# A two-block transformer kernel: the first expert's tokens gathered by column halves, second-bias products moved behind expert two, a down-projection unit's parts moved ahead of conditioning work

## The reference

```
def swiglu(x, w_up, w_down):                      # feed-forward of the first block
    a, b = split(x @ w_up, 2)
    return (silu(a) * b) @ w_down

def moe_ffn(h, w_router, b_router, w1, b1, w2, b2):   # 32 experts, 4 for each token
    logits = h @ w_router + b_router
    top_v, top_e = top_k(logits, 4); weights = softmax(top_v)
    for each expert e and the tokens sent to it:
        hcat  = x[tok] @ w1[e] + b1[e]            # 1024 -> 2048
        act   = min(glu, 7) * sigmoid(1.702 * glu) * (clip(lin, -7, 7) + 1)
        y     = act @ w2[e] + b2[e]               # 1024 -> 1024
    out = sum over the 4 experts of weights * y
```

## Time and profile before

| | us |
|---|---|
| median of 3 runs | 2614.63 |
| lowest and highest of them | 2614.07, 2614.64 |
| the profiled execution | 2615.32 |
| span of its instructions | 2613.6 |
| PE busy | 2581.9 |
| DVE busy | 1295.6 |
| moved from and to HBM | 705 MB, mean 270 GB/s |

### The profile page before, as it was taken

How to read it: one execution, slowest core, us unless ns; L and a number is a source line. 1 busy time by engine, 2 the same in 40 slices (tenths; PEclk the granted TensorE clock), 3 DMA queues, 4 the chain that set the end, 5 groups by cost and what they waited for, 6 DMA issues and landing times.

```text
span 2613.6 us, 39337 instructions
## 1 busy us (share of the span) xinstructions
PE 2581.9 (99%) x15833; PEld 1899.0 (73%) x15833; DVE 1295.6 (50%) x1741; ACT 759.0 (29%) x1288; POOL 73.7 (3%) x95
## 2 busy tenths in 40 slices
PE   9999999999999999999999999999999999999998
PEld 9989898999999998999989888833333333333333
DVE  6866785687788768747844063312122121112112
ACT  4414441443343245323423143122121121121111
POOL 0010200000000120000001000000000000000000
PEclk9999999999999999999999999999999999999999
DMA  6685433456656834445554533899999999999999
GB/s 231 212 283 184 140 138 145 161 178 223 222 191 205 301 129 133 152 152 164 186 198 149 206 107 151 328 392 426 427 428 427 428 427 427 428 428 427 427 428 406
DMA packets 265659, 705.38 MB, mean 270 GB/s; under 512 B 13125, under 2 KB 155409, under 8 KB 215761
## 3 DMA queue, kind: packets, MB, share of 16 engines
q1 hardware_dynamic: 253520, 663.66, 65.9%
q0 software_dynamic: 9856, 36.41, 3.9%
q10 hardware_dynamic: 2176, 3.83, 0.4%
HBM read 699.61 MB, written 6.60 MB: 270 GB/s over the span
## 4 chain that ended last, share of the span: by engine, by line
PE 77%; SPq 12%; DMA 7%; DVE 2%; issue 1%; ACT 1%; DVEq 0%; ACTq 0%
PE acc L1824 8%; SPq L917 8%; PE acc L1089 6%; PE mix L1093 6%; PE acc L1091 6%; PE acc L1035 5%; PE acc L1162 5%; PE acc L1839 4%; PE acc L1629 4%; SPq L920 4%; PE mix L1083 4%; PE acc L1178 3%; PE acc L1061 2%; PE acc L1112 2%; PE acc L1421 2%; DMA big<-in_w 2%
## 5 line engine op out<-in xcount | busy, mean ns | idle before, releaser
L1089 PE MATMUL acc<-branch_parts,area_parts 128*128 128x256 f32 x1176 | 343.9, 292 | 0.4 <-DVE big_parts L2436 0.4
L1093 PE MATMUL mix<-big_parts,zz_parts 128*128 128x256 f32 x1176 | 332.8, 283 | 0.0
L1091 PE MATMUL acc<-area_parts,ring_parts 128*128 128x256 f32 x1176 | 332.4, 283 | 0.0
L3256 DVE COPY zz<-acc 128x512 f32<-128x512 f32 x32 | 22.1, 692 | 546.4 <-PE acc L1824 546.4
L2436 DVE TENSOR_TENSOR ring_parts<-ring,area_parts 128x1792 fp32r<-128x1792 f32 (+2 forms) x125 | 238.0, 1904 | 84.2 <-ACT area_parts L1982 61.0
L1089 PEld LDWEIGHTS acc<-branch_parts,area_parts 128*128 128x128 f32 x1176 | 225.0, 191 | 9.7 <-DVE big_parts L2436 1.2
L1091 PEld LDWEIGHTS acc<-area_parts,ring_parts 128*128 128x128 f32 x1176 | 225.1, 191 | 0.2
L1093 PEld LDWEIGHTS mix<-big_parts,zz_parts 128*128 128x128 f32 x1176 | 225.0, 191 | 0.0
L1982 ACT ACTIVATE area_parts<-ring 128x1792 fp32r<-128x1792 f32 (+1 forms) x116 | 189.6, 1634 | 16.6 <-DMA ring<-in_ffn_up 12.1
L2529 DVE SCALAR_TENSOR_TENSOR zz_parts<-area_parts,ring_parts 128x1792 fp32r<-128x1792 f32 x84 | 170.2, 2026 | 6.3
L1974 ACT ACTIVATE area<-acc 128x256 f32<-128x256 f32 (+1 forms) x66 | 32.5, 492 | 367.6 <-PE acc L1776 341.6
(11 more groups left out here) (553 smaller groups left out, 4740.2 us busy)
## 6 DMA issues: line engine op xcount, KB each, us to landing
ring<-in_ffn_up SPq DMA_DIRECT2D x86, 1024.0 KB, 5.0
big<-in_w SPq DMA_DIRECT2D x79, 1024.0 KB, 25.7
ring<-in_w SPq DMA_DIRECT2D x76, 1024.0 KB, 26.0
ring<-in_w_in SPq DMA_DIRECT2D x72, 1024.0 KB, 7.1
area<-in_w SPq DMA_DIRECT2D x57, 1024.0 KB, 26.3
spare<-in_w SPq DMA_DIRECT2D x38, 1024.0 KB, 25.6
area<-in_w_ada POOLq DMA_DIRECT2D x24, 1024.0 KB, 7.7
ring<-in_ffn_down SPq DMA_DIRECT2D x28, 768.0 KB, 4.7
```

Source lines behind the costliest of these rows:

```text
L1089: pe.matmul(abank(a, b)[:, ts], wg[:, b, k, c * P:c * P + P], xg[:, k, :], start=c == 0 and k == 0, stop=False, skip_group_check=True)
L1091: pe.matmul(abank(a, b)[:, ts], wl[:, k, c0:c0 + P], xl[:, k, :], start=False, stop=k == K - 1, skip_group_check=True)
L1093: mm = pe.matmul(kbank(a, b)[:, ts], wk[:, b, k, c * P:c * P + P], xk[:, k, :], start=False, stop=k == K - 1, skip_group_check=True)
```

## The change

1. `gather(1)` and `gather_turn(1)` are replaced by `first_gather(c)` for the column halves c = 0, 1, into the two hidden banks `H_BANK[c]`. ACT copies each half by itself, PE turns each half (two transposes into `X_BANK`, two into `Y_BANK`), and ACT's first tokens wait for the half that they need. The counts of the semaphores `rows_gathered`, `rows_copied` and `x_gathered` go up by one for all later gathers.
2. The four zero products leave the place in front of the loop: three of them take the place of two of three filler products ahead of the gather, the fourth stands behind the second half's gather.
3. `add_b2` does chunk 0 ahead of the turns, chunks 1 and 2 behind them, and chunks 3 to 7 after the down products of expert one, which follow expert two's up units.
4. In `swiglu`, for all experts, DVE adds the first bias to both banks, and clamps and multiplies after that.
5. In the routing, DVE's conversion of the indices stands ahead of the negated maximum.
6. In the down projections, unit 3's parts are made earlier: ACT makes units 0 to 3 ahead of squares 0 and 1, and units 4 and 5 ahead of squares 2 and 3; DVE makes unit 3's remainders ahead of conditioning piece 2, not behind it.

```diff
             pe.wait_ge(htm_ready, 4)
-            idle_products(abank(G_WOUT2 + 1, 0), 3)
+            for n in range(1, 4):
+                zeros(n)
+            idle_products(abank(G_WOUT2 + 1, 0), 1)
...
+            def first_gather(c):
+                for b in range(NB):
+                    for half in range(2):
+                        c0 = half * 512 + c * T
+                        mm = pe.matmul(H_BANK[c][64 * half:64 * half + 64, 0:T], sel[:, b, :], htm[:, b, c0:c0 + T],
+                                       start=b == 0, stop=b == NB - 1)
+                mm.then_inc(rows_gathered, 1)
+            def first_turn(c):
+                pe.wait_ge(rows_copied, 2 + c)
+                for j in range(2):
+                    g0 = c * T + j * P
+                    mm = pe.transpose((X_BANK, Y_BANK)[c][:, j * P:j * P + P], g_slot[:, g0:g0 + P], ident)
+                mm.then_inc(x_gathered, 1)
...
-            gather(1)
-            gather_turn(1)
+            pe.wait_ge(sel_ready, 1)
+            for c in range(2):
+                first_gather(c)
+            zeros(0)
+            first_turn(0)
             after(pe, wgt_ready)
...
+            first_turn(1)
             pe.wait_ge(round_ready, 1)
...
-            for n in range(4):
-                pe.matmul(mix[:, n, 0:1], ident, zero, start=True, stop=False, skip_group_check=True)
             with pe.Fori(0, rounds) as q:
...
-                add_b2(q, 0, 3)
+                add_b2(q, 0, 1)
                 turn(first, 0)
                 turn(first, 1)
-                add_b2(q, 3, DC)
+                add_b2(q, 1, 3)
                 slots_free(first + 1)
...
                 down_between(1, 16)
+                add_b2(q, 3, DC)
...
-                        for u in ((0, 1, 2), (3, 4), (5,))[m // 2]:
+                        for u in ((0, 1, 2, 3), (4, 5), ())[m // 2]:
                             down_upper(L, n // 2, u)
...
+                    if g == 1:
+                        down_lower(L, s, 3)
                     for at, j in enumerate(ada):
                         ada_half(8 * ADA_STAGES.index((L, a0)) + j)
-                        if at == 0 and g:
-                            down_lower(L, s, 2 * g + 1)
+                        if at == 0 and g == 2:
+                            down_lower(L, s, 5)
...
                        bias1.unsqueeze(2).to_broadcast([P, 8, C_SLOT]), ALU.add).then_inc(h_read, 1)
-                    v.drain()
+                v.drain()
+                for a in range(2):
                     g, lin = glu[:, a, 0:T], glu[:, a, T:2 * T]
```

More of the change, by code:

```diff
@@ L1764, in _, with zeros @@
             pe.wait_ge(htm_ready, 4)
-            idle_products(abank(G_WOUT2 + 1, 0), 3)
+            def zeros(n):
+                pe.matmul(mix[:, n, 0:1], ident, zero, start=True, stop=False, skip_group_check=True)
+            for n in range(1, 4):
+                zeros(n)
+            idle_products(abank(G_WOUT2 + 1, 0), 1)
             def gather(it):
@@ L2374, in _, with token, first_tokens @@
             g.then_inc(gexp_ready, 1)
+            def token(k, bank, at):
+                act.activation(x_slot[:, k, :], bank[:, at:at + C_SLOT], ACT.Identity,
+                               bias=mod[:, 24 + k:25 + k], scale=gains[:, 1, k:k + 1]).then_inc(x_slot_ready, 1)
+            def first_tokens():
+                for k, part in ((0, 0), (1, 0), (2, 1), (3, 1), (4, 0), (5, 0), (6, 1), (7, 1)):
+                    act.wait_ge(x_gathered, 1 + part)
+                    token(k, (X_BANK, Y_BANK)[part], (2 * (k % 2) + k // 4) * C_SLOT)
             def tokens(g):
-                act.wait_ge(x_gathered, g)
+                act.wait_ge(x_gathered, g + 1)
                 for k in range(DC):
                     at = (2 * (k % 4) + k // 4) * C_SLOT
-                    c = act.activation(x_slot[:, k, :], X_BANK[:, at:at + C_SLOT], ACT.Identity,
-                                       bias=mod[:, 24 + k:25 + k], scale=gains[:, 1, k:k + 1])
-                    c.then_inc(x_slot_ready, 1)
+                    token(k, X_BANK, at)
             def rows(g):
-                act.wait_ge(rows_gathered, g + 1)
+                act.wait_ge(rows_gathered, g + 2)
                 copy(g_slot, X_BANK).then_inc(rows_copied, 1)
@@ L2413, in down_done @@
                 copy(y, Y_BANK).then_inc(y_copied, 1)
-            rows(1)
-            tokens(1)
+            for c in range(2):
+                act.wait_ge(rows_gathered, 2 + c)
+                copy(g_slot[:, c * T:c * T + T], H_BANK[c][:, 0:T]).then_inc(rows_copied, 1)
+            first_tokens()
             after(act, wT_done)
-            copy(wT[0:EXPERTS, :], Y_BANK[0:EXPERTS, 0:T]).then_inc(wT_ready, 1)
+            copy(wT[0:EXPERTS, :], Y_BANK[0:EXPERTS, T:2 * T]).then_inc(wT_ready, 1)
             act.wait_ge(round_ready, 1)
@@ L2656, in down @@
                     if not len(ada):
-                        for u in ((2,), (3, 4), (5,))[g]:
+                        for u in ((2,), (4,), (5,))[g]:
                             down_lower(L, s, u)
@@ L3288, in _ @@
                 first, used = q * EXPERTS, q * UNITS_Q
-                v.wait_ge(x_gathered, first + 1)
+                v.wait_ge(x_gathered, first + 2)
                 slots_of(slice(1, 2))
@@ L3292, in _ @@
                 with v.Fori(1, EXPERTS) as e:
-                    v.wait_ge(x_gathered, first + e + 1)
+                    v.wait_ge(x_gathered, first + e + 2)
                     slots_of(bass.ds(e + 1, 1))
```

6 lines of the change are left out of this document (3 added, 3 removed).

## The result

| | before | after |
|---|---|---|
| median, us | 2615.86 (20 runs, 2612.93 to 2620.25) | 2621.38 (20 runs, 2614.64 to 2625.25) |
| the profiled execution, us | 2615.32 | 2621.06 |
| its span, us | 2613.6 | 2619.3 |

The ratio is 1.0017, with an interval of 1.001 to 1.0025: slower, by 4.4 us by the ratio and 5.5 by the medians, where 1.3 us less was forecast; the median lies above the range. The profiled executions differ by 5.7 us. To see where, I took one mark that both traces have, DVE's copy of the row means in each layer norm (`lnmu<-mix`). After, it comes 0.2 us later up to layer 0's second down projection, 5.6 us later behind that one, 9.8 us later behind layer 1's first and up to the routing, and the end comes 5.7 us later. So in these two executions the stages of edit 6 lost 5.4 and 4.2 us, and what follows gained 4.0.

A forecast was written before the change was run, and what follows sets the result against it. PE was taken to bound the kernel before the expert stage, the DMA weight stream within it. Gains of 1.3 and 2.5 us less a 2.5 us loss made -1.3 us: 2614.6 to 2613.3 us, range 2611.5 to 2615.3.

The forecast's parts named there:

- The second bias: Expert one to two: moved bias products and earlier adds start unit 8 2.1 us earlier, gaining 2.5 us (2.0 to 2.5).
- second hole: Expert weight stream, 1723 to 1732 us: 307 instead of 427 GB/s, 2.5 us lost.
- The first gather: Before expert one: halved gather and moved zero products start unit 0 1.3 us earlier (0.7 to 1.6), all gained.
- first hole: Expert weight stream, 1700 to 1710 us: 307 instead of 427 GB/s, 2.8 us lost.
- the loop's entry: PE before unit 0: loop start-up, formerly hidden by the zero products, may show; 0.2 us, at most 0.8.
- Edit 5: Routing, DVE reorder: gains nothing; depending on the clock, up to 1 us earlier or later.
- The expert stage as a whole: First gather and second bias together: 3.8 us gained (2.7 to 5.3).
- Edit 6, the gain: Conditioned down projections: PE's 1.2 us wait at unit 3 goes but returns at unit 5; zero gain in both layers.
- Edit 6, the price: Conditioned down projections: piece 4, requested later, delays DVE and PE by 1.4 us in layer 0, 1.1 in layer 1; 2.5 lost.
- the same landing time: Piece 4, issued 2.6 us later, still takes 6.9 us (layer 0) and 6.1 us (layer 1) to land.
- ACT holds the squares: Rival: unit 5's late landing delays ACT's squares, 2.9 us more in layer 1; total 2617 to 2618 us; chance 0.16.
- the piece lands in time: Rival: piece 4 lands in 5 us or less, so edit 6 costs nothing; 2610.8 us, or 2609.3; chance 0.28.

The follow-up runs named there:

- e12: Kernel before with only the second-bias split and both bias adds ahead of the clamps; 2614.18 us, ratio 0.9988.
- e2: Changed kernel with the down-projection reorder (unit 3's parts earlier) undone, all other edits kept; 2613.13 us, ratio 0.9988.
- e3: Kernel before with only DVE's part of the down-projection reorder, ACT's order kept; 2619.98 us, ratio 1.0015.
- e9: Changed kernel, six later conditioning pieces per stage cut from 1 MB to 256 KB (conditioning vector wrong); 2612.78 us, ratio 0.9983.
- e10: Changed kernel without the down-projection reorder, six later conditioning pieces per stage cut to 256 KB; 2611.03 us, ratio 0.9979.
- e1: Kernel before with only the down-projection reorder, both DVE's and ACT's parts; 2623.65 us, ratio 1.0026.
- e13: Changed kernel with eight useless PE products ahead of the wait for unit 5's parts in two down stages; 2618.98 us, ratio 1.0006.
- e14: Changed kernel, six later conditioning pieces per stage cut from 1 MB to 512 KB (conditioning vector wrong); 2611.95 us, ratio 0.9986.
- e7: Changed kernel with each conditioning piece loaded and given back in two halves; 2623.35 us, ratio 1.0025.
- e8: Changed kernel without the down-projection reorder, each conditioning piece loaded and given back in two halves; 2613.24 us, ratio 0.9987.
- e6: Changed kernel run again unchanged, since the condition for its intended filler products never held; 2621.69 us, ratio 1.0018.
- e4: Changed kernel with unit 5's remainders also moved ahead of conditioning piece 5 on DVE; 2624.39 us, ratio 1.0031.

## Why the prediction was wrong, step by step

- **The second bias** (2.5 us, second hole closed): right. Unit 8 came 2.9 us after unit 7's end and 2.1 us earlier, both as forecast, and the second hole is closed.
- **The first gather** (1.3 us): the first hole is 1.5 us after, as forecast, but unit 0 came only 0.8 us earlier, and the hole alone proves nothing (1.8 in e12, without this edit). The step that failed is the loop's entry, taken at 0.2 us and at most 0.8: PE's last turn ended at 1706.67 + 0.38 = 1707.05, 3.0 us behind the gather's start as the prediction has it, and unit 0 began at 1707.78, 0.7 later. The row's bracket names ACT's tokens, since one of them ended just then. But PE waits there only for the first of the eight, whose semaphore the trace has at 1707.07. PE's sequencer is at the number of rounds and the loop's registers until 1707.7. In the kernel before that lay under the zero products.
- **Edit 5** (nothing, ends of 1 us): in the profiled execution the gather came 1.2 us sooner behind the last layer norm, since the clock did not fall in the routing. But in e2, with the same edit, it fell there again and the gather took the 296.3 us of the kernel before, and in e3 and e12, without the edit, it did not fall and the gather took 295.1. So this belongs to the execution, not to the edit.
- **The expert stage as a whole** (3.8): 4.0 in the profiled executions, 1.2 of it that clock; 2.6 by the medians of e2, 2.2 from the gather on by the means of the profiles. The forecast was too high by 1.2 to 1.6 us, 0.5 of it the first gather's. (Its upper end, 5.3, is both holes whole; the ends of its two terms add up to 4.1.)
- **Edit 6, the gain** (zero): right. e9 and e10 show it when nothing else is in the way. (The prediction's list of PE's waits lacks one, 0.7 us at unit 3 of layer 1, at 867.12; it goes too, and is met again at unit 5.)
- **Edit 6, the price** (2.5): this step failed, 9.6 us in the profiled executions and 7.9 in e1. It took "the same landing time" for piece 4, from one row each, 6.9 and 6.1 us, in a stretch where the engines are busy nearly all the time. There a landing time is no constant: the same piece 3 took 5.9 us in the kernel before and 9.0 in e12. The kernel before had been profiled in an execution where DVE waited for no landing between piece 2 and unit 5's parts in layer 0; e2 and e12, with the same order upstream, waited 3.4 and 2.6 us at unit 5 there. By the 7.9 of e1, an estimated 1.7 us of the 9.6 is that execution's luck. The forecast counted one late piece per stage; layer 0 had two (1.6 + 1.5), layer 1 one (2.1) and the squares (1.0 more than the usual 0.5).
- **A term that was left out: the clock.** The forecast had PE's wait at unit 5 grow above 1 us and gave it the length of the wait. Behind the waits of some 4 us the clock was at 1.2 GHz here: 5.4 us lost in layer 0 for parts 3.0 us late, 4.2 in layer 1 for parts another 2.9 late. By e13 this share is roughly 3 us of the whole.
- **Rivals.** "ACT holds the squares" was the right kind, in layer 1, with 1 us of its 2.9. That the piece lands in time was the weightiest rival, and the wrong way. The Trainium skill's figure ("DMA: Bandwidth & Descriptors", Anatomy of one DMA), 4.4 us for 1 MB by the estimate in the prediction, is below every row of the loaded stages: behind the first two of each stage, whole pieces took 5.3 to 9.8 us in the eleven profiles that have them. With the load taken away, 256 KB landed in 3.5 us.

Open is why ACT's part alone costs as much as DVE's. It may be that both make the unit's and the pieces' requests fall together differently, but that is not shown: which transfer is late differs from execution to execution, and one profile of each does not show a rule. Nor was it seen why a late transfer is late.

## What to carry to other kernels

Read the DMA share, not the rate, of the stretch in which you move work: at the 0.94 to 0.97 of these stages a landing time read from one execution is a draw, not a price, and a reorder that takes the slack away from a landing pays for the late ones. Read it from several profiles: here the first one of the kernel before was a lucky one. When one wait only turns up at another place (unit 3, unit 5, the sums), look for the resource that they share, and take load off it in an experiment before moving more work. And price a PE wait of some us with the slower products behind it.

## What the runs showed of the hardware

- A 1 MB transfer, asked for within 0.5 us of the same moment behind the same order of work, landed after 5.9 us (kernel before) and 9.0 us (e12), at DMA shares of 0.97 and 0.95; one of 640 KB, asked for at 651.3 and 651.2, after 7.3 and 9.9 in the same two. With a share of 0.7 to 0.8 it took 5.5 (e9) and 5.1 us (e14), and the pieces, there smaller, 3.5 (256 KB) and 5.2 us (512 KB).
- DMA engines can be busy 0.94 to 0.97 of the time at 315 to 333 GB/s, where the experts' stream reaches 427.
- Asking for a transfer in two halves, the first sooner, brought that transfer in sooner (piece 4 of layer 0 by 1.3 us in e7) while another one was later (unit 5's by 1.9 us), and the time did not fall.
- TensorE's clock fell to 1.2 GHz, for 3.4 or 6.8 us, behind waits of PE in these two stages as short as 1.9 us (e8) and as long as 5.5 us (e6), and stayed at 2.4 GHz behind waits of 3.0 us (e2) and 3.1 us (e4). In e13, where products of no use filled 3.6 us of each wait, it stayed up in both.
